# RWKV's output gate projection, moved from the delta net's first direction into the second

## The reference, cut to what matters

```
proj = x @ w_in
dn_qkv, dn_ab, dn_gate, rk_in, rk_gate = jnp.split(proj, EVEN_SPLITS, axis=-1)
...
o = gated_delta_chunked(q, k, v, g[0], beta[0]) + flip_l(
    gated_delta_chunked(flip_l(q), flip_l(k), flip_l(v), flip_l(g[1]), flip_l(beta[1])))
y_dn = o.astype(x.dtype) * jax.nn.silu(dn_gate)
...
s = bidir_token_shift(rk_in, rk_mu).astype(f32)
...
wkv = rwkv7_scan(r, w_f, k, v, a_vec, b_vec) + flip_t(
    rwkv7_scan(flip_t(r), flip_t(w_b), flip_t(k), flip_t(v), flip_t(a_vec), flip_t(b_vec)))
...
y_rk = (wkv + bonus).astype(x.dtype) * jax.nn.silu(rk_gate)
return jnp.concatenate([y_dn, y_rk], axis=-1)
```

## Time and profile before

| | |
|---|---|
| median of 3 runs | 1756.61 us |
| lowest and highest | 1754.81 and 1759.01 us |
| span of the profiled execution | 1757.2 us |
| TensorE busy | 1620.6 us (92%) |
| VectorE busy | 1127.0 us (64%) |
| ScalarE busy | 780.1 us (44%) |
| mean granted TensorE clock | 0.938 of full speed |

### The profile page before, as it was taken

The page is one execution under the profiler, slowest core; times in us unless marked ns, Lnnn a source line. Parts: engine busy times, 40 slices in busy tenths (PEclk is TensorE's granted clock), DMA queues, the critical chain, the costliest instruction groups (busy, mean ns, idle before and its releaser), DMA issues.

```text
span 1757.2 us, 24313 instructions
## 1 busy us (share of the span) xinstructions
PE 1620.6 (92%) x10180; PEld 1419.7 (81%) x10180; DVE 1127.0 (64%) x1910; ACT 780.1 (44%) x1320; POOL 55.7 (3%) x52
## 2 busy tenths in 40 slices
PE   7998998999989989989999899878799899999897
PEld 6988887999879888879998888766688777885465
DVE  5586557555555765465555669455787658976676
ACT  4556345444444554354444474222312226645245
POOL 0000011000000000100000001000000000000000
PEclk9999999999999999899999989976798789999999
DMA  8553334655545533246555633000002045431143
GB/s 258 166 170 110 116 120 156 207 186 182 184 135 179 163 115 103 98 155 203 191 178 175 204 120 96 1 1 0 1 1 97 1 165 186 144 120 37 48 125 109
DMA packets 151182, 219.95 MB, mean 125 GB/s; under 512 B 6230, under 2 KB 110686, under 8 KB 150432
## 3 DMA queue, kind: packets, MB, share of 16 engines
q1 hardware_dynamic: 151072, 218.39, 38.8%
HBM read 217.31 MB, written 1.06 MB: 124 GB/s over the span
## 4 chain that ended last, share of the span: by engine, by line
PE 75%; DVE 15%; ACT 6%; DMA 2%; issue 1%; SPq 0%; DVEq 0%
PE bank L385 18%; PE bank L386 17%; PE bank L387 17%; DVE weights_low L361 4%; PE bank L2052 4%; PE bank L884 3%; PE bank L2143 2%; PE bank L3379 2%; ACT weights_high L348 2%; PE bank L2338 2%; DVE place L2532 1%; PE bank L2109 1%; PE bank L3340 1%; DMA place<-ple_gate_dram 1%; DMA place<-w_in_dram 1%
## 5 line engine op out<-in xcount | busy, mean ns | idle before, releaser
L361 DVE TENSOR_TENSOR weights_low<-place,weights_high 128x1024 fp32r<-128x1024 f32 (+2 forms) x387 | 448.0, 1201 | 185.4 <-ACT weights_high L348 185.3
L348 ACT ACTIVATE weights_high<-place 128x1024 fp32r<-128x1024 f32 (+2 forms) x387 | 378.5, 1031 | 136.7 <-DMA place<-w_down_dram 42.8
L385 PE MATMUL bank<-hT_high,weights_high 128*128 128x256 f32 x1152 | 336.7, 292 | 5.0 <-DVE hT_low L482 4.0
L387 PE MATMUL bank<-hT_high,weights_low 128*128 128x256 f32 x1152 | 328.7, 285 | 0.0
L386 PE MATMUL bank<-hT_low,weights_high 128*128 128x256 f32 x1152 | 327.7, 284 | 0.0
L385 PEld LDWEIGHTS bank<-hT_high,weights_high 128*128 128x128 f32 x1152 | 221.2, 192 | 11.1 <-DVE hT_low L482 5.2
L386 PEld LDWEIGHTS bank<-hT_low,weights_high 128*128 128x128 f32 x1152 | 221.6, 192 | 0.6
L387 PEld LDWEIGHTS bank<-hT_high,weights_low 128*128 128x128 f32 x1152 | 220.5, 191 | 0.0
L2052 PE MATMUL bank<-place,place 128*128 128x128 f32 x624 | 92.6, 315 | 25.4 <-DVE place L2499 9.0
L2052 PEld LDWEIGHTS bank<-place,place 128*128 128x128 f32 x624 | 88.4, 227 | 32.7 <-issue 21.7
L386 PE MATMUL bank<-weights_low,branchT_high 128*128 128x512 f32 x256 | 101.7, 397 | 0.0
(11 more groups left out here) (427 smaller groups left out, 3326.0 us busy)
## 6 DMA issues: line engine op xcount, KB each, us to landing
place<-w_in_dram SPq DMA_DIRECT2D x48, 1024.0 KB, 5.3
place<-w_up_dram SPq DMA_DIRECT2D x32, 1024.0 KB, 5.5
place<-w_down_dram SPq DMA_DIRECT2D x32, 1024.0 KB, 5.0
place<-even_w_in_dram SPq DMA_DIRECT2D x17, 1024.0 KB, 5.2
place<-w_out_dram SPq DMA_DIRECT2D x16, 1024.0 KB, 5.2
place<-odd_w_in_dram SPq DMA_DIRECT2D x16, 1024.0 KB, 5.4
place<-w_branch_dram SPq DMA_DIRECT2D x12, 1024.0 KB, 5.0
place<-ple_gate_dram SPq DMA_DIRECT2D x8, 1024.0 KB, 6.1
```

What stands on the lines that cost most here:

```text
L348: nc.scalar.activation(high[:, lo:hi], self.raw[p % SLOTS][:, lo:hi], ACT.Copy).then_inc(*A("high", p, j))
L361: nc.vector.tensor_tensor(low[:, lo:hi], self.raw[p % SLOTS][:, lo:hi], high[:, lo:hi].bitcast(FP32), ALU.subtract).then_inc(*V())
L385: nc.tensor.matmul(out, left[0], right[0], start=first, stop=False)
L387: return nc.tensor.matmul(out, left[1], right[0], start=False, stop=last)
```

## The change

RWKV's gate is taken out of the filler of direction 0 on all three engines. Direction 1 gets it as a second filler, `gate`, on TensorE: a quarter behind the beta group of each chunk, one ahead of `rows_tensor`, and the last (`gate.finish()`) behind the prepared parts and ahead of the levels. ScalarE's two Silus stand at that last place. The ring stays at 6 until then and only then becomes 8.

```diff
--- before.py
+++ after.py
@@ -2153,7 +2153,7 @@
         for m0 in (0, 2):
             k.pair(("conv", part, m0), ("conv", part, m0), e.hT, h_ready)
     k.ring = 6
-    fill = Filler(silu_tensor(k, e, "dn"), shifted_tensor(k, e), silu_tensor(k, e, "rk"))
+    fill = Filler(silu_tensor(k, e, "dn"), shifted_tensor(k, e))
     k.token_major(("ab",), [(("ab",), KT)], e.hT, DN_AB, h_ready)
     squares = split(e.squares, 4, S)
     for _ in l2_tensor(k, e, ("q",), squares, table("ones")[:, 0:1]):
@@ -2164,9 +2164,8 @@
     tokens_tensor(k, ("v",), e.qkvT[:, 2], fill, ("conv_silu", 2, 2))
     delta_tensor(k, e, 0, fill)
     fill.finish()
-    k.ring = 8
-    fill = Filler(prepared_tensor(k, e))
-    delta_tensor(k, e, 1, fill)
+    fill, gate = Filler(prepared_tensor(k, e)), Filler(silu_tensor(k, e, "rk"))
+    delta_tensor(k, e, 1, fill, gate)
     fill.finish()
     rwkv_tensor(k, e)
     for t in CLOSE_ORDER[0]:
@@ -2175,7 +2174,7 @@
         w_out_tensor(k, 0, e.close, t)
 
 
-def delta_tensor(k, e, d, fill):
+def delta_tensor(k, e, d, fill, gate=None):
     nc, T, table = k.nc, k.T, k.table
     incl, g, beta = k.inclusive(d), e.g(d), e.beta(d)
     for name, left in (("Gc", incl), ("Gsum", table("ones"))):
@@ -2193,12 +2192,18 @@
             four_tensor(k, (name, d, c), lambda h: e.qkvT[:, 1, h, cut], lambda h: e.qkvT[:, right, h, cut], ("l2_done", "k"))
         four_tensor(k, ("beta", d, c), lambda h: beta[:, c, h:h + 1].to_broadcast([P, P]), lambda h: table("ident"))
         if d:
+            gate()
             fill()
     inv = ("dn", d)
     if d == 0:
         fill(3)
+    else:
+        gate()
     rows_tensor(k, e, e.inverse_dn, inv, d)
     fill(4 if d else 5)
+    if d:
+        gate.finish()
+        k.ring = 8
     for i in range(len(LEVELS) - 1):
         level_tensor(k, e, e.inverse_dn, inv, i)
     rhs4, U4, work4 = (split(a, 4, P) for a in (e.rhs, e.U, e.work))
@@ -2534,7 +2539,7 @@
     nc.vector.tensor_tensor(e.mu_c, e.mu[:, 0, :], e.mu[:, 1, :], ALU.add).then_inc(*V())
     V.wait_ge(V)
     nc.vector.tensor_scalar(e.mu_c, e.mu_c, -1.0, 1.0, ALU.mult, ALU.add).then_inc(*V("mu_made"))
-    fill = Filler(silu_vector(k), shifted_vector(k, e), silu_vector(k, False))
+    fill = Filler(silu_vector(k), shifted_vector(k, e))
     k.low_of_next()
     delta_sums_vector(k, e)
     for _ in l2_vector(k, e, ("q",), e.qkvT[:, 0], None, table("ones")[:, 0:1], P ** -0.5):
@@ -2992,8 +2997,7 @@
                 nc.scalar.activation(squares, e.qkvT[:, 0], ACT.Square).then_inc(*A("squares", "q"))
             A.wait_ge(("conv_done", part, m0))
             nc.scalar.activation(e.qkvT[:, part, m0:m0 + 2, :], e.qkvT[:, part, m0:m0 + 2, :], ACT.Silu).then_inc(*A("conv_silu", part, m0))
-    fill = Filler(silu_scalar(k, e, "dn", e.silu_dn), shifted_scalar(k, e),
-                  silu_scalar(k, e, "rk", e.silu_rk, ("shifted_done", 5), ("shifted_done", 6)))
+    fill = Filler(silu_scalar(k, e, "dn", e.silu_dn), shifted_scalar(k, e))
     k.high_of_next()
     A.wait_ge(("even_loaded",))
     for t in range(TT):
@@ -3038,6 +3042,9 @@
     fill(2 if d else 3)
     rows_scalar(k, e.inverse_dn, ("dn", d), d)
     fill(4 if d else 5)
+    if d:
+        for _ in silu_scalar(k, e, "rk", e.silu_rk, ("shifted_done", 5), ("shifted_done", 6)):
+            pass
     for i in range(len(LEVELS) - 1):
         level_scalar(k, e.inverse_dn, ("dn", d), i)
     for step in range(TT):
```

## The result

The changed kernel takes 1740.06 us (median of 4 runs, 1737.91 to 1741.98), before 1755.71 in the same job: a ratio of 0.9901 (95% interval 0.9886 to 0.9917), 15.7 us faster. The forecast was 1750.0, 6.6 us faster, with a range from 1744 to 1758.5: right in sign, too small by more than half, and outside the range. Later jobs gave the changed kernel 0.9924 (0.9894 to 0.9954) and 0.9919 (0.9889 to 0.9948); the median of its 17 runs is 1740.4, and they spread from 1734.7 to 1754.1.

What follows compares the result with a forecast made beforehand. TensorE was taken as the bound (busy 92% of the span), with gate quarters needlessly in direction 0's relay. A 2.8, B 2.2, C 0.9 and D 0.7 sum to 6.6 us, giving a median of 1750.0; range 1744 to 1758.5.

Steps and rivals of the forecast that it cites:

- A: Step 1 of direction 0: the relay without gate quarters ends earlier, though at half clock; 2.8 us gained (0.5 to 7.8).
- R3: Rival, larger gain: direction 0's relay keeps full clock; gain 11.6 us or more, time 1745; chance 0.14.
- B: Direction 1, quarter before L2075: fits the 3.28 us idle and speeds the groups behind; 2.2 us gained (-1.2 to 3.0).
- C: Direction 1, two quarters before the rows group: hidden behind VectorE, rows group faster; 0.9 us gained (-4.1 to 1.75).
- D: Direction 1, last quarter before the levels: hidden, levels at full clock, less a Silu wait; 0.7 us gained (-0.7 to 1.6).
- R1: Rival, slower: quarters run at half clock and overrun direction 1's gaps; 1760 to 1762 us; chance 0.12.
- R2: Rival, no change: direction 0's uncovered relay falls to half clock and stays there; gain 1.7, 1755 us; chance 0.19.

Runs made afterwards that it cites:

- rep_after: The changed kernel repeated with only a constant added at the end of the file; 1748.4 us (1 run).
- again_after: The changed kernel repeated with only a constant added at the end of the file; median 1740.7 us (6 runs).
- fourth_after: The changed kernel repeated for a fourth profile, with only a constant added at the end of the file; median 1739.5 us (6 runs).
- extra: The kernel before plus 12 products that nobody reads ahead of direction 1's levels; 1757.8 us, ratio 1.0004 to the kernel before.
- relay_extra: The changed kernel plus five units of three unread products in the relay of direction 0's step 1; 1736.3 us, ratio 0.9887 to the kernel before.
- bank: The changed kernel with the turn set to bank 0 when the ring goes back to 8; 1746.2 us, ratio 0.9949 to the kernel before.

## Why the prediction was wrong

The mechanism was right: the quarters left a serial relay and went where TensorE waited. The sum was 6.6; the stretch gave 9.7 in the first profile, and 3.9 more came right behind it. What failed is the pricing of the clock behind the relay and behind the dense quarters: too low in the terms of the sum, and put at nothing, without a reason, for step 0 of direction 1. The terms below are measured on the first profile.

- **A, 2.8 taken, 5.2 measured** (legs to rhs, o and decay, 24.9 to 19.7). This is the term that was mis-sized most. The rhs came 2.1 to 2.2 earlier, as worked out, the relay ran at half clock from the first solve on, nearly as taken, and Gsum's wait went. Measured from the token shift, o started 4.5 earlier for the 4.0 worked out, and with 3.46 for 3.78 o and qS ended 3.1 earlier for 2.3. The larger part lies behind: the forecast left the decays as they were, like a_lora, which did stay (1.99). Before, the decays had run at 0.56 of full clock, after a dense stretch; now they ran at 1.00, 2.05 us for 3.46. I had allowed for full clock there only as part of the far upper end (R3), bound to a relay at full clock. It needs no such relay. Nor is it sure: rep_after and again_after give 5.2 as well, fourth_after only 1.1, with a_lora and decays at half clock.
- **B, 2.2 taken, 0.6 measured** (leg to beta, 14.1 to 13.6). The quarter fitted, as taken, but the expected full clock behind it did not come: AT and NT took 3.44. L2075 to beta gave 1.6, and 1.0 went again as VectorE waited 1.13 for the Exp that A had brought into view. In fourth_after the full clock did come (2.03), and B was 3.3.
- **C, 0.9 taken, 2.2 measured** (leg to L2832). The two quarters fitted, and the rows group took 3.81: the full gain that I had halved, and the last prepared product behind it (the second L2234) took 1.53 for 2.01. In fourth_after C was 4.0; A, B and C together were 8.0 in the first profile and 8.4 there, for the 5.9 taken.
- **D, 0.7 taken, 1.7 measured**, in all four profiles. The levels went to full clock, the upper end. The 0.7 us taken off for the Silu did not come: the quarter took 4.4 us and not 5.1, and the Silu, 0.6 behind it, ended with VectorE's transpose.
- **Step 0 of direction 1, not in the sum, 3.9.** I followed the dense quarter's effect for 3.55 us, to the point where TensorE had warmed up before, and not to the next place where the clock had fallen. extra, with 15.0 for the 18.9 of two profiles of before in three, speaks for the quarter as the cause.
- **RWKV's units, 4.9 between the two profiles.** Not the change's by any run here, nor excluded: 150.7 to 159.3 among four profiles of the same kernel. The range had no room for such draws; it was made of the stretch's terms alone.

The rivals: R1 fails, as all quarters ran at full or nearly full clock in the first two gaps and left idle time. R2 had the right picture of the relay, in fourth_after of a_lora and decays too, and the wrong one of what follows: B, C and D were no smaller for it. R3 came nearest (1745) for the wrong reason: the relay did lose its clock. The weighing of what the Trainium skill says ("TensorE: Matmul & The Clock Gate", Part 1: how busy the array has recently been sets the clock) against the 22 us of half clock at full busy time came out between the two: the last quarter took 4.42 us (1194.36 to 1198.78), part at half clock and part at full, so the clock came back within it. In relay_extra too it rose within the quarter, in extra and bank only at its end; during the small matmuls that fill 1179 to 1201 it did not, in any profile of before.

## What to carry to other kernels

In a serial relay of small matmuls, a filler longer than the wait is paid in full; put long fillers where TensorE waits for a long chain of another engine, and cut the ones in a relay to the length of its waits. Price a dense filler by what it does to the clock of the groups behind it too, and follow that effect past the next fall of the clock: here 15 unread products in waits made the kernel no slower and its stretch, in the one profile, 3.3 us shorter, and 36 products removed made it slower. And time legs between the same instructions in several profiles of the same kernel before a difference is given to a change: the total held draws of 9 us in a stretch that nobody touched.

## What the runs showed of the hardware that I had not expected

- The clock of the same instructions differs from one execution to the next by place, and costs whole microseconds: RWKV's units took 150.7 to 161.6 us over the profiles, step 0 of direction 1 15.0 or 18.7 to 18.9 with nothing in between.
- In all profiles of before the granted clock was 0.50 from 1179 on while TensorE was busy without a gap. With 12 dense products behind them full clock began within these or at their end (changed kernel, extra), and then held through step 0 (1.00), over waits of up to 1.5 us.
- The place of the half clock can move with little effect on a whole stretch: a_lora and the decays took 4.0 or 7.6 us together, AT and NT of chunk 1 3.4 or 2.0, and the stretch 84.2 or 83.9 (first profile and fourth_after).
